# Three-unit stage openings, heads first, and the last square of a post norm summed on TensorE

## What is computed

```python
# block 1                                   (stages 1 and 2 of the kernel)
z = rmsnorm(x) @ w_in                       # then four mixers: rwkv7, mlstm, window attention, forgetting attention
x = x + rmsnorm(mix(z) @ w_out)
gate, up = split(rmsnorm(x) @ ffn_w_up)     # 2 x 2816 columns
x = x + rmsnorm((gelu(conv(gate)) * up) @ ffn_w_down)
# block 2                                   (stages 3, 4, 5; 6 is the last norm)
x = x + 0.5 * swiglu(rmsnorm(x), ...)       # 2816 wide
x = x + mixer(rmsnorm(x))                   # gated linear attention and a convolution
x = x + 0.5 * swiglu(rmsnorm(x), ...)
return rmsnorm(x)
```

## Time and profile before

| | value |
|---|---|
| median of 3 runs | 1740.0 us |
| the profiled execution, its own time | 1741.66 us |
| its span in the profile | 1739.8 us |
| TensorE (PE) busy | 1654.2 us, 95% |
| VectorE (DVE) busy | 820.3 us, 47% |
| ScalarE (ACT) busy | 697.7 us, 40% |
| GpSimd (POOL) busy | 289.2 us, 17% |
| mean granted TensorE clock | 0.981 |

### The profile page before, as it was taken

How to read it: one execution, slowest core, us unless ns; L and a number is a source line. 1 busy time by engine, 2 the same in 40 slices (tenths; PEclk the granted TensorE clock), 3 DMA queues, 4 the chain that set the end, 5 groups by cost and what they waited for, 6 DMA issues and landing times.

```text
span 1739.8 us, 21730 instructions
## 1 busy us (share of the span) xinstructions
PE 1654.2 (95%) x8578; PEld 1338.9 (77%) x8578; DVE 820.3 (47%) x1276; ACT 697.7 (40%) x1255; POOL 289.2 (17%) x241
## 2 busy tenths in 40 slices
PE   6999998988999999979999999999999999999995
PEld 5776776667888888858888888878887788888884
DVE  4566344355655542255444433367455444444332
ACT  5556445545433333245333332244533433333222
POOL 1221110023222210022222210000010122222001
PEclk9999998989999999999999999999999999999998
DMA  4220011121332233313222323322132232232331
GB/s 166 85 74 26 14 49 37 58 100 61 110 97 97 97 93 98 100 49 109 97 97 97 97 88 101 103 80 86 37 101 83 72 112 96 99 97 93 98 100 58
DMA packets 44133, 148.37 MB, mean 85 GB/s; under 512 B 5064, under 2 KB 6144, under 8 KB 44032
## 3 DMA queue, kind: packets, MB, share of 16 engines
q1 hardware_dynamic: 40032, 140.53, 24.9%
q10 hardware_dynamic: 4000, 6.46, 1.1%
HBM read 144.86 MB, written 2.10 MB: 84 GB/s over the span
## 4 chain that ended last, share of the span: by engine, by line
PE 87%; DVE 6%; ACT 5%; issue 1%; POOL 1%; DMA 0%; DVEq 0%; ACTq 0%; POOLq 0%
PE bank L198 76%; PE bank L335 6%; PE bank L304 3%; DVE t L170 3%; ACT t L158 2%; DVE t L180 2%; ACT L158 1%; PE bank L206 1%; DVE t L261 1%; ACT t L257 1%; POOL t L170 1%; DVE t L184 0%; DMA t<-in_cst 0%; DVE t L190 0%; ACT t L165 0%
## 5 line engine op out<-in xcount | busy, mean ns | idle before, releaser
L198 PE MATMUL bank<-t 128*128 128x512 f32 (+6 forms) x7578 | 1516.3, 360 | 26.8 <-DVE t L170 10.0
L198 PEld LDWEIGHTS bank<-t 128*128 128x128 f32 (+3 forms) x7578 | 1161.1, 179 | 296.8 <-issue 36.8
L261 DVE TENSOR_TENSOR t<-t 128x512 fp32r<-128x512 f32 (+1 forms) x516 | 394.3, 795 | 436.4 <-ACT t L257 428.8
L170 POOL TENSOR_TENSOR t<-t 128x512 f32<-128x512 f32 (+1 forms) x181 | 239.4, 1322 | 1210.0 <-DVE t L170 563.3
L257 ACT ACTIVATE t<-t 128x512 fp32r<-128x512 f32 (+1 forms) x540 | 310.7, 613 | 261.2 <-PE bank L335 216.9
L158 ACT ACTIVATE t<-t 128x512 f32<-128x512 f32 (+6 forms) x351 | 202.6, 605 | 357.7 <-DVE t L170 169.6
L170 DVE TENSOR_TENSOR t<-bank,t 128x512 f32<-128x512 f32 (+4 forms) x238 | 147.4, 630 | 237.2 <-PE bank L335 213.7
L335 PE MATMUL bank<-t 128*128 128x512 f32 x516 | 200.7, 389 | 0.0
L165 ACT ACTIVATE t<-t 128x512 fp32r<-128x512 f32 (+3 forms) x87 | 51.7, 606 | 250.0 <-POOL t L170 247.6
L170 DVE TENSOR_TENSOR t<-t 128x512 f32<-128x512 f32 (+7 forms) x135 | 96.6, 733 | 72.2 <-ACT t L158 62.0
L180 DVE SCALAR_TENSOR_TENSOR t<-t 128x512 f32<-128x512 f32 (+3 forms) x142 | 104.0, 748 | 39.7 <-ACT t L158 38.3
(11 more groups left out here) (22 smaller groups left out, 90.0 us busy)
## 6 DMA issues: line engine op xcount, KB each, us to landing
t<-in_ffn_w_up SPq DMA_DIRECT2D x88, 512.0 KB, 4.4
t<-in_w_in SPq DMA_DIRECT2D x50, 512.0 KB, 3.5
t<-in_ffn_w_down SPq DMA_DIRECT2D x48, 512.0 KB, 3.5
t<-in_ffn_w_gate SPq DMA_DIRECT2D x44, 512.0 KB, 3.4
t<-in_ffn_w_down SPq DMA_DIRECT2D x24, 384.0 KB, 3.1
t<-in_w_out SPq DMA_DIRECT2D x16, 512.0 KB, 3.5
t<-in_xt SPq DMA_DIRECT2D x8, 256.0 KB, 5.9
t<-in_xt ACTq DMA_DIRECT2D x8, 256.0 KB, 4.6
```

The source lines that it names most:

```text
L170: return q.do(lambda e: e.tensor_tensor(out, a, b, op), *deps, us=self.cost(out, q, True))
L198: fn = lambda e: e.matmul(out, w, x, start=start, stop=stop, skip_group_check=True)
L261: q.put(lambda e: e.tensor_tensor(lo, raw, hi.bitcast(F), SUB), self.s_tail[i % 2], 1, (self.s_head, i + 1), before, us=0.79 if q is self. ...
```

## The change

Every opening now goes through `Stream.open`, which multiplies three units side by side: for each tile k first head by head of all three, then weight tail by head; the 24 products with input tails come last. Since the six cut buffers are all in use, each has a semaphore of its own. `add_post` is rewritten to run on VectorE alone and to make all heads before the tails. The last square of a post norm is summed by a third product with ones on its own, and the other two sums are written inside the last product. In `pre_norm`, the additions of squares all go to VectorE (`own=True`).

```diff
-        self.s_head, self.s_used = sem("s_head"), sem("s_used")
+        self.s_head = sem("s_head")
+        self.s_used = [sem(f"s_used{n}") for n in range(CUT)]
...
+    def used(self, i):
+        return (self.s_used[i % CUT], i // CUT + 1)
...
+    def open(self, outs, xh, heads, xl, *free):
+        pe, at = self.p.pe, self.at
+        part = lambda t, u, k: t[(at + 2 * u + k // 4) % CUT][:, (k % 4) * 128:(k % 4) * 128 + 128]
+        self.ahead(CUT)
+        for k in range(8):
+            for u, out in enumerate(outs):
+                i = at + 2 * u + k // 4
+                self.p.mm(out, part(self.hi, u, k), xh[k], k == 0, False, heads[k], (self.s_head, i + 1), *free)
+            for u, out in enumerate(outs):
+                self.p.mm(out, part(self.lo, u, k), xh[k], False, False, self.tail(at + 2 * u + k // 4))
+        for k in range(8):
+            for u, out in enumerate(outs):
+                fn = lambda e, o=out, w=part(self.hi, u, k), x=xl[k][0], z=k == 7: e.matmul(
+                    o, w, x, start=False, stop=z, skip_group_check=True)
+                if k % 4 == 3:
+                    pe.put(fn, self.used(at + 2 * u + k // 4)[0], 1, xl[k][1], us=0.227)
+                else:
+                    pe.quiet(fn, xl[k][1], us=0.227)
+        self.at += 2 * len(outs)
+        return [self.used(at + 2 * u + 1) for u in range(len(outs))]
...
     def product(self, W, banks, xh, xl):
         if self.rms:
-            two = [banks.next(), banks.next()]
-            m = W.pair([b.t[:, :] for b in two], xh, xl, *[b.free for b in two])
-            self.done = list(zip(two, m))
-            yield
-            self.third = W.parts(self.extra.t[:, :], 1, xh, xl, self.extra.free)
-            next(self.third)
+            three = [banks.next(), banks.next(), self.extra]
+            m = W.open([b.t[:, :] for b in three], xh, W.p.heads, xl, *[b.free for b in three])
+            self.done = list(zip(three, m))
             self.rms()
             self.rms = None
+            yield
...
-            q, sum_, last = (p.dv, acc2, "acc2") if k % 2 else (p.po, acc, "acc")
+            q, sum_, last = (p.dv, acc2, "acc2") if k % 2 else (p.dv if own else p.po, acc, "acc")
...
+        def sums(b):
+            p.mm(b.t[:, :], ones, acc[:, :], True, False, state["acc"], b.free)
+            state["acc_read"] = p.mm(b.t[:, :], ones, acc2[:, :], False, False, state["acc2"], last=True)
+        def rest(b, src, *deps):
+            a = p.act(sq[1][:, :], src, ACT.Square, state["sq"][1], *deps)
+            state["sq"][1] = m = p.mm(b.t[:, :], ones, sq[1][:, :], False, True, a, last=True)
+            W.ahead(CUT - 1)
+            b.free, state["rB"] = rstd_of(b.t[:, :], 1.0 / 1024, eps[:, 0:1], rB[:, :], m, state.get("rB_read"))
+            return a
...
                     if f == 0:
-                        mg, mu = W.pair([bg.t[:, :], bu.t[:, :]], xh, xl, bg.free, bu.free)
-                        early = W.product(bank[2].t[:, :], 1, xh, xl, bank[2].free)
+                        three = [bg, bu, bank[2]]
+                        mg, mu, early = W.open([b.t[:, :] for b in three], xh, p.heads, xl, *[b.free for b in three])
                         p.rms()
...
-        def add_post(then, y, yt, b):
-            W.ahead(CUT)
-            finish_norm(b)
-            heads = []
+        def add_post(then, y, yt):
             for n in range(8):
                 a = p.tt(y[n][:, :], y[n][:, :], rB[:, :], MUL, yt[n], state["rB"])
-                xtok[n] = p.tt(xt[n][:, :], xt[n][:, :], y[n][:, :], ADD, a, xtok[n], q=p.dv if n % 4 == 0 else p.po)
-                heads.append(head(n, then))
-                if n:
-                    made[n - 1] = tail(n - 1, then, heads[n - 1])
-            made[7] = tail(7, then, heads[7])
+                xtok[n] = p.tt(xt[n][:, :], xt[n][:, :], y[n][:, :], ADD, a, xtok[n])
+                begun[n] = head(n, then)
+                if n == 1:
+                    W.ahead(CUT)
+            for n in range(8):
+                made[n] = tail(n, then, begun[n])
```

More of the change, by code:

```diff
@@ L1 @@
+import itertools
 import math
@@ L1636, in pre_norm @@
             for k in range(8):
-                if made[k] is None:
-                    made[k] = tail(k, gain, head(k, gain))
+                if begun[k] is None:
+                    begun[k] = head(k, gain)
+                    made[k] = tail(k, gain, begun[k])
             W.ahead(CUT)
@@ L1699, in ffn @@
                 yt = []
+                if post:
+                    log_table()
                 for n in range(8):
                     b = bank[4 + n % 2]
[L1702 to L1705, removed]
+                    g = W.parts(b.t[:, :], 3, [t[:, :] for t in fH],
+                                [(fL[i][:, :], fl[i]) for i in range(22)], b.free)
+                    m = ended(g, 3, (lambda: sums(bank[6])) if post and n == 7 else None)
+                    if post and n == 7:
+                        yt.append(add_last(y[n], post, b, m, bank[6]))
+                    elif post:
+                        square_in(n, b.t[:, :], m, own=n == 6)
                         b.free = t = p.act(y[n][:, :], b.t[:, :], ACT.Copy, m, scale=col(post, n))
@@ L1715, in ffn, with ended, add_last @@
                 if post:
-                    add_post(then, y, yt, bank[6])
+                    add_post(then, y, yt)
                 yx.close()
-        def add_post(then, y, yt, b):
-            W.ahead(CUT)
-            finish_norm(b)
-            heads = []
+        def ended(g, n, then):
+            for i in itertools.count(1):
+                try:
+                    next(g)
+                except StopIteration as end:
+                    return end.value
+                if i == n and then:
+                    then()
+        def add_last(y, post, b, m, into):
+            a = rest(into, b.t[:, :], m)
+            b.free = t = p.ts(y[:, :], b.t[:, :], col(post, 7), None, MUL, None, a)
+            return t
+        def add_post(then, y, yt):
             for n in range(8):
                 a = p.tt(y[n][:, :], y[n][:, :], rB[:, :], MUL, yt[n], state["rB"])
-                xtok[n] = p.tt(xt[n][:, :], xt[n][:, :], y[n][:, :], ADD, a, xtok[n], q=p.dv if n % 4 == 0 else p.po)
-                heads.append(head(n, then))
-                if n:
-                    made[n - 1] = tail(n - 1, then, heads[n - 1])
-            made[7] = tail(7, then, heads[7])
+                xtok[n] = p.tt(xt[n][:, :], xt[n][:, :], y[n][:, :], ADD, a, xtok[n])
+                begun[n] = head(n, then)
+                if n == 1:
+                    W.ahead(CUT)
+            for n in range(8):
+                made[n] = tail(n, then, begun[n])
             state["rB_read"] = a
@@ L1743, in project_out @@
                         b = bank[n % 2]
-                        m = W.product(b.t[:, :], 1, xh, xl, b.free)
-                    if post:
-                        square_in(n, b.t[:, :], m)
+                        m = ended(W.parts(b.t[:, :], 1, xh, xl, b.free), 1,
+                                  (lambda: sums(bank[2])) if post and n == 7 else None)
+                    if post and n == 7:
+                        yt.append(add_last(y[n], post, b, m, bank[2]))
+                    elif post:
+                        square_in(n, b.t[:, :], m, own=n == 6)
                         b.free = t = p.act(y[n][:, :], b.t[:, :], ACT.Copy, m, scale=col(post, n))
@@ L1756, in project_out @@
                 if post:
-                    add_post(then, y, yt, bank[2])
+                    add_post(then, y, yt)
         def done_all():
```

43 lines of the change are left out of this document (16 added, 27 removed).

## The result

The changed kernel takes 1787.36 us (4 runs, 1786.98 to 1788.49) against 1740.58 before: 1.0269 times as long, 95% interval 1.0251 to 1.0287, 46.8 us slower. The forecast was 1782.5, between 1768 and 1792. The profiled execution took 1786.98, its span is 1785.2.

A forecast was written before the change was run, and what follows sets the result against it. TensorE, 87% of the last-ending chain, was taken as the bound. First opening +10.0, stage 2 +3.5, stage 3 +4.5, stage 4 +9.7 and stage 5 +14.8 gave +42.5: 1782.5 us on the median, range 1768 to 1792.

The forecast's parts named there:

- The pauses behind the norm: After each opening's sum with ones, TensorE waits for weights cut behind the norm's chain: 10.06, 10.75, 8.9, 5.5, 8.8 us.
- The rival without pauses: TensorE finds its next pieces ready after the sum, so the five pauses never come: 1736 us, chance 0.04.
- The hold of the first tile: Stages 4 and 5: the opening's first tile waits for the third unit's first weight tail, until 1134.05 and 1362.55.
- The gain behind a post norm: Stages 2 and 3: the sum with ones ends 28.7 after the old end, not 35.2 and 34.9; gain 6.5 and 6.2.
- VectorE's chain: Openings of stages 2 and 3: tails and squares take 20.8 us, ending just as TensorE's products do.
- The shared ports: add_post: VectorE operations with two SBUF inputs and GpSimd ones take a shared port pair in turn, so additions pay on VectorE.
- the lone figure: add_post: three VectorE operations alone take 2.02 us, so 16 cost 10.8, against up to 28 by the pace beside GpSimd.
- The clock: Behind each new pause TensorE loses 1.8 us to a lower clock, bounds 0 and 2.8; half for stage 4's hold.
- The table load costed at nothing: Ln's table load ahead of the output products, 1.28 us, lies under TensorE's products; uncovered it is 1.3 twice.
- The cover that I named: TensorE's products have four pieces in hand, 10.9, which hide Ln's table load ahead of the output products.
- The first mixer: First opening: the fourth unit starts 8.2 us later, at 43.95 instead of 35.73; with 1.8 for the clock +10.0.
- my rival: Mixers swallow part of their loss in later waits for VectorE's chains, half of 20: 1772 us, chance 0.15.

The follow-up runs named there:

- experiment 3: Changed kernel, the third unit's first weight piece split right behind the last product of stages 3 and 4: 1777.61 us, 1.022 of the kernel before.
- experiment 7: Three-unit openings only behind post norms, later Ln table load, six of eight add_post additions of x back on GpSimd: 1736.41 us, 0.9981 of the kernel before.
- experiment 9: experiment 5 plus six useless float32 products behind each post norm's last sum with ones: 1731.71 us, 0.9957 of the kernel before.
- experiment 10: experiment 5 with the sixth weight piece cut ahead of Ln, not behind add_post's second tile: 1730.93 us, 0.9943 of the kernel before.
- experiment 11: experiment 10 plus the six useless products of experiment 9 in each post norm's pause: 1729.73 us, 0.9944 of the kernel before.
- experiment 1: Changed kernel plus one line: open writes the splits of four more weight pieces behind its products; 1751.02 us, 1.0059 of the kernel before.
- experiment 5: Changed kernel with three-unit openings only behind post norms, four pieces cut behind them, other openings as before: 1731.2 us, 0.9952 of the kernel before.
- experiment 5 again: The kernel of experiment 5 unchanged, run once more beside experiment 9: 1731.73 us, 0.9951 of the kernel before.
- experiment 2: Changed kernel with twelve useless float32 products behind the sum with ones in the three FFN openings: 1782.23 us, 1.0244 of the kernel before.

## Why the prediction was right, point by point

**The pauses behind the norm** are the change's price, and shown: measured against forecast they are 10.15 against 10.06 in the first mixer, 10.65 against 10.75 in stage 2, 8.71 against 8.9 in stage 3, 5.31 against 5.5 in stage 4 and 8.71 against 8.8 in stage 5. Their size was read off the same chain in the trace of before, since no instruction of it changed. One line that restores the cut takes 36.3 us off. The rival without pauses counts them as "44 with their clock"; 44 is their length alone.

**The hold of the first tile** in stages 4 and 5 is shown by experiment 3. The rows gave its end right: in stage 5 the third unit's first weight tail is done 8.0 after the last product's end, as forecast, and in stage 4 it is 3.5, as forecast. TensorE starts a little earlier than the forecast had it, since what releases its dense part is that piece's head (1391.14, 6.9 after the last product's end).

**The gain behind a post norm** was over-sized, 6.5 and 6.2 forecast, 5.5 and 5.1 measured at the end of the sum. Two terms were off, and end at the same moment. VectorE's chain, put at 20.8, took 22.0, from 386.67 to 408.68, because the weight tail put behind the second tile stood 1.31 for a ScalarE head (row 390.72 in experiment 7). TensorE's own 72 products, put at 18.5 with 1.8 for the clock, took 19.2 in stage 2 (388.89 to 408.13) without a wait. Experiments 9 to 11 show that to cure one of the two gains next to nothing at the sum, and both gain 2.0. The pace I read, 0.67 an operation, held.

**The shared ports.** The weighing came out for the lone figure. The Trainium skill, "SBUF — State Buffer", on who interferes with whom, is borne out in its direction: an operation took 0.67 alone and 1.08 on average beside GpSimd. The 4.8 us for two openings is not the ports' alone, as experiment 7 says.

**The clock**, 1.8 a pause, was right in kind and near in size: each group of eleven behind a pause lost time. In order they are 2.2, 2.3, 1.7, 1.6 and 2.4 (4.88, 4.96, 4.32, 4.28 and 5.06 less 2.65), and stage 5 goes on at 3.09 for the next. A term that I left out is at the first opening, whose 46 products took 12.60, 2.2 more than at full rate. Stage 4 has 1.1 more that was not forecast: behind a pause of 2.92 near its end, which both kernels have, eleven products and the next eleven took 5.37 and 3.06 in this profile; before, they took 4.79, with a wait of 0.46 in it, and 2.67.

**The table load costed at nothing** cost 1.1, behind the first mixer. The cover that I named, four pieces in hand, was not what was waited for: TensorE waited for a bank that ScalarE had to empty, and ScalarE had eight DMA issues and then the load ahead of it.

**The first mixer: partly luck.** The start of the mixer is +9.7 at its fourth unit, and with the slow clock behind that pause it grows to +12.5, more than the +10.0 forecast. It falls to +7.4 at the mixer's end, and the table load behind it makes that about the 8.7 of the table. Of what was given back, 3.1 is one stretch of 75 small products and 1.6 another, of 27 (timeline of PE, before and after):

```profile
207.53 13.73 PE L198 MATMUL bank<-t 64*64 64x64 f32 x75 [1.16 <-ACT t L165]
...
257.34 7.74 PE L198 MATMUL bank<-t 32*128 32x512 f32 x27
```
```profile
220.00 10.61 PE L199 MATMUL bank<-t 64*64 64x64 f32 x75 [1.18 <-ACT t L166]
...
266.67 6.16 PE L199 MATMUL bank<-t 32*128 32x512 f32 x27
```

The wait ahead is the same, so it is not the chains that caught up, as my rival had it. The granted clock had a low stretch in both places before (0.80 over 205 to 222, 0.86 over 255 to 267) and none after. Nothing ties this to the change: experiments 1 and 3, which open the first mixer as the changed kernel does, have the first stretch slow as well (13.75 and 13.74). Nor is it the position in the span: experiments 5 and 9 are the same program up to the first post norm and reach this stretch within 0.05 us of each other, and yet (experiment 5, then 9):

```profile
207.81 10.60 PE L199 MATMUL bank<-t 64*64 64x64 f32 x75 [1.20 <-ACT t L166]
```
```profile
207.76 13.74 PE L199 MATMUL bank<-t 64*64 64x64 f32 x75 [1.20 <-ACT t L166]
```

The second stretch took 7.75 in experiment 5 and 6.16 in experiment 5 again, one and the same kernel. So one execution differs from another here, and the profile of before was taken of one with both stretches slow. What brings them on is open. Without them the first line of the table would be about +13.4 (an estimate, 8.7 + 3.1 + 1.6), so its nearness to +10.0 is in good part luck.

## What to carry to other kernels

When engines run in the order written, look at what a rewritten opening no longer writes behind itself: here one missing call put the next weights behind a norm, and pauses of 9 to 11 us in the FFNs hid gains of 5 behind each post norm. A wider opening pays where inputs come slowly and the norm behind it is covered; elsewhere the third unit was that cover. And before curing a clock or a wait, find the second chain that ends at the same moment: two cures that each did next to nothing gave 2 us together at their place. Then look at the next wait in the stage, where most of it was lost again.

## What the runs showed of the hardware

Plain float32 products into an unused bank held the granted clock through pauses of 4.9 and 8.7 us: in stage 3, 1.00 instead of 0.76 over 804 to 812. In stage 2 they left the last 2.91 of the pause open, and the clock fell. The Trainium skill, "TensorE: Matmul & The Clock Gate", Part 1, says that activity releases the throttle, and experiments 2 and 9 agree. Less expected was that the same code, in programs that do not differ ahead of it, can lose 3.1 us at a place in one execution and nothing in another (experiments 9 and 5). Behind equal waits of 2.6 to 2.7 for a weight tail eleven products took 2.79 in experiment 10, 3.87 in experiment 1 and 4.38 in experiment 11. So a difference of that size between two profiles is no proof of a cause nearby.
